# Order of side steps and evictions, gate softplus, compressed attention and the 2o3 turnover in a two-block kernel

## The reference, cut to what matters

```python
p_cmp = jax.nn.softmax(jnp.where(cmp_mask, s_cmp, NEG_INF), axis=-1) * cmp_mask
o_cmp = jnp.einsum('bhgsi,bihd->bshgd', p_cmp.astype(v_cmp.dtype), v_cmp)
o = g[..., 0, :] * o_cmp + g[..., 1, :] * o_sel + g[..., 2, :] * o_win
dt = jax.nn.softplus(dt_raw.astype(jnp.float32) + dt_bias.astype(jnp.float32))
h = h + mixed @ w_out[l]
h = h + (jax.nn.silu(v @ w_gate[l]) * (v @ w_up[l])) @ w_down[l]
```

```python
x = x + rms_norm(merged @ w_o[l], norm_mix_post[l])
h = rms_norm(x, norm_ffn_pre[l])
gate, up = jnp.split(h @ w_ffn_in[l], 2, axis=-1)
x = x + rms_norm((jax.nn.silu(gate) * up) @ w_ffn_down[l], norm_ffn_post[l])
```

## Time and profile before

| what | value |
|---|---|
| three runs, us | 2635.20, 2635.26, 2635.38; median 2635.26 |
| profiled execution, us | 2636.87, of which the profile's span is 2635.1 |
| TensorE (PE) | busy 2617.9 us, 99% of the span |
| VectorE (DVE) | busy 1483.2 us, 56% |
| ScalarE (ACT) | busy 1238.9 us, 47% |
| granted TensorE clock, mean | 0.999 |
| moved by DMA | 483.97 MB, 184 GB/s |

### The profile page before, as it was taken

One profiled execution on the slowest core, in us unless ns is written; L12 is line 12 of the kernel. 1 busy time (PEld: TensorE's weight loads), 2 busy tenths in 40 slices (PEclk: granted clock), 3 DMA queues, 4 the chain that ended last, 5 costly groups with the idle time before them and its releaser, 6 DMA issues.

```text
span 2635.1 us, 33219 instructions
## 1 busy us (share of the span) xinstructions
PE 2617.9 (99%) x13670; PEld 2238.4 (85%) x13670; DVE 1483.2 (56%) x1792; ACT 1238.9 (47%) x1577; POOL 0.2 (0%) x4
## 2 busy tenths in 40 slices
PE   9999999999999999999999999999999999999998
PEld 9989788888888888899899888888788888888887
DVE  6676765545454545566567644556655444555456
ACT  5565545443444444465454454444554444443443
POOL 0000000000000000000000000000000000000000
PEclk9999999999999999999999999999999999999999
DMA  8534445565555655556544435565565565565554
GB/s 306 164 122 144 151 148 199 189 191 193 191 188 191 193 193 187 191 182 211 185 157 154 151 130 190 185 234 187 167 211 186 192 194 189 191 191 192 190 193 144
DMA packets 132039, 483.97 MB, mean 184 GB/s; under 512 B 14704, under 2 KB 14960, under 8 KB 130832
## 3 DMA queue, kind: packets, MB, share of 16 engines
q1 hardware_dynamic: 131744, 481.70, 55.7%
q10 hardware_dynamic: 144, 0.15, 0.0%
HBM read 477.20 MB, written 4.19 MB: 183 GB/s over the span
## 4 chain that ended last, share of the span: by engine, by line
PE 98%; DVE 1%; ACT 1%; issue 0%; DVEq 0%
PE ps L415 96%; PE ps L419 2%; ACT W L989 0%; DVE W L1483 0%; DVE W L1886 0%; DVE scr L1483 0%; DVE wlo L1483 0%; DVE h L1486 0%; ACT whi L989 0%; ACT L989 0%; ACT xhi L989 0%; DVE xlo L1486 0%; ACT sm L989 0%; DVEq L2339 0%; DVE sm L1483 0%
## 5 line engine op out<-in xcount | busy, mean ns | idle before, releaser
L1483 DVE TENSOR_TENSOR wlo<-raw,whi 128x1024 fp32r<-128x1024 f32 x886 | 1082.1, 1223 | 1007.0 <-ACT whi L989 1002.9
L989 ACT ACTIVATE whi<-raw 128x1024 fp32r<-128x1024 f32 x886 | 935.7, 1058 | 1140.8 <-PE ps L415 1129.2
L415 PE MATMUL ps<-whi,xlo 128*128 128x512 f32 x2080 | 816.7, 393 | 0.0
L415 PE MATMUL ps<-wlo,xhi 128*128 128x512 f32 x2080 | 810.4, 390 | 0.0
L415 PE MATMUL ps<-whi,xhi 128*128 128x512 f32 x2080 | 810.3, 390 | 0.0
L415 PEld LDWEIGHTS ps<-wlo,xhi 128*128 128x128 f32 x2080 | 390.8, 188 | 82.0
L415 PEld LDWEIGHTS ps<-whi,xlo 128*128 128x128 f32 x2080 | 391.0, 188 | 79.8 <-issue 0.5
L415 PEld LDWEIGHTS ps<-whi,xhi 128*128 128x128 f32 x2080 | 391.0, 188 | 79.6 <-issue 0.5
L415 PE MATMUL ps<-whi,hlo 128*128 128x512 f32 x944 | 370.5, 392 | 0.0
L415 PE MATMUL ps<-wlo,hhi 128*128 128x512 f32 x944 | 367.5, 389 | 0.0
L415 PE MATMUL ps<-whi,hhi 128*128 128x512 f32 x944 | 367.3, 389 | 0.0
(11 more groups left out here) (130 smaller groups left out, 1013.2 us busy)
## 6 DMA issues: line engine op xcount, KB each, us to landing
raw<-in_gu SPq DMA_DIRECT2D x352, 512.0 KB, 3.8
raw<-in_w_in SPq DMA_DIRECT2D x256, 512.0 KB, 3.6
raw<-in_dn SPq DMA_DIRECT2D x176, 512.0 KB, 3.8
raw<-in_w_out SPq DMA_DIRECT2D x32, 512.0 KB, 3.6
raw<-in_w_up SPq DMA_DIRECT2D x32, 512.0 KB, 3.5
raw<-in_w_o SPq DMA_DIRECT2D x32, 512.0 KB, 3.9
raw<-in_cmp SPq DMA_DIRECT2D x8, 512.0 KB, 3.5
W<-in_wb SPq DMA_DIRECT2D x3, 1024.0 KB, 6.1
```

Of the source, the lines that this page charges most:

```text
L415: return e.matmul(o, l, r, start=start, stop=stop, skip_group_check=skip)
L989: return e.activation(o, i, f, **kw)
L1483: return e.tensor_tensor(o, a, b, op)
```

## The change

1. `walk()` on ScalarE and VectorE: the side step comes ahead of `after()` and `tick()`, no longer behind them. TensorE's `walk` keeps its order. Fox starts one step later on all three (`+ 6`).
2. `attention_T()` begins with an empty step on all three engines, and its transposes wait for `s_crd` 4 where it was 5; all that follows in the chain (`ssd`) is a step later.
3. `gates()`: 24 ticks pass between dt and softplus.
4. `compressed()`: the probabilities are multiplied with `t` in steps 5 and 6 (one more operation of 128x240), and in steps 9 and 10 the values in PSUM are added to `att_o` in one operation where there were two.
5. The turnover: `post(2, 0)` and `post(2, 1)` are issued in `turnover()` at tb 1, ahead of `quads_lo`; `posts()` keeps column block 3. The transposes of column blocks 2 and 3 move from behind units 0 and 2 of tb 1 to behind units 1 and 3.
6. The eviction of an `1x` item waits for `s_taps` as well.

```diff
@@ tensor, between_2fg0
-                elif (tb, u) in ((1, 0), (1, 2)):
+                elif (tb, u) in ((1, 1), (1, 3)):
                     c = 2 + u // 2
@@ tensor, attention_T (scalar and vector: the same yield)
             def attention_T():
+                yield
                 for k in range(0, 8, 2):
-                    tiles_T("h", HF["mix"] + k, 1024 + k * 128, scr, (s_crd, 4 + 1))
+                    tiles_T("h", HF["mix"] + k, 1024 + k * 128, scr, (s_crd, 4))
@@ tensor, scalar, vector: fox
-                while done[0] < end["2bf"] + 5:
+                while done[0] < end["2bf"] + 6:
@@ scalar and vector, walk
                         split_to(ahead(it["first"] + u))
                         done[0] += 1
+                        if side is not None:
+                            next(side, None)
                         if u == it["n"] - 1:
                             after(nm, it, pair_of(i))
                         tick()
-                        if side is not None:
-                            next(side, None)
@@ scalar, gates (vector: the same line ahead of its softplus)
                 m.then_inc(s_gs, 1)
+                yield from later(24)
                 yield from softplus(1, 32, 1)
@@ vector, after
                     on.wait_ge(s_tap0, 4 * n)
+                    on.wait_ge(s_taps, n)
                     mine()
@@ vector, turnover
                     if tb:
                         m.then_inc(ev["2o3"][0], 1)
+                        post(2, 0)
+                        post(2, 1)
@@ vector, compressed
-                        tt(ex, ex, bc(C("cmul")[:, tb * 15:tb * 15 + 15], 1, [P, 16, 15]), MUL).then_inc(s_cp, 1)
+                        own.up(tt(ex, ex, bc(C("cmul")[:, tb * 15:tb * 15 + 15], 1, [P, 16, 15]), MUL))
+                        mine()
+                        tt(ex, ex, bc(t, 2, [P, 16, 15]), MUL).then_inc(s_cp, 1)
...
-                            tt(rt, B("co", tb, gp).rearrange("p (h d) -> p h d", h=8), bc(t16c[tb][:, 8 * gp:8 * gp + 8], 2, [P, 8, 64]), MUL).then_inc(s_crd, 1)
-                            on.wait_ge(s_crd, 2 * tb + gp + 1)
-                            m = tt(att_o(tb, gp), att_o(tb, gp), rt, ADD)
-                            if (tb, gp) == (1, 1):
-                                m.then_inc(s_crd, 1)
-                            else:
-                                own.up(m)
+                            tt(att_o(tb, gp), att_o(tb, gp), B("co", tb, gp).rearrange("p (h d) -> p h d", h=8), ADD).then_inc(s_crd, 1)
@@ vector, posts
-                for c in (2, 3):
-                    post(c, 0)
-                    post(c, 1)
+                post(3, 0)
+                post(3, 1)
                 yield
```

More of the change, by code:

```diff
@@ L1925, in compressed @@
             def compressed():
-                rt = RT.rearrange("p (h d) -> p h d", h=8)
                 for i in range(11):
```

## The result

The changed kernel takes 2626.2 us (median of six runs, 2626.08 to 2626.36); the kernel before, run beside it, 2635.33 (six runs, 2635.20 to 2636.86). The ratio is 0.9962, 95% interval 0.9952 to 0.9973. The profiled executions took 2626.27 and 2636.87, with spans of 2624.5 and 2635.1.

A forecast was written before the change was run, and what follows sets the result against it. TensorE was taken to bound the kernel; 4.1 + 1.34 + 1.51 + 2.0 + 1.32 - 0.1 = 10.2 us off gave 2626.7 from the profiled 2636.87 and 2625.1 from the median 2635.26, range 2623.9 to 2629.2.

The forecast's parts named there:

- PE bounds, 8.0 us can go: Whole kernel: TensorE is busy 2617.9 of 2635.1 us; only 8.00 us of waits in five windows can go.
- The turnover, 4.1: Window 1888 to 1910: early posts remove PE's wait for h, 2.22 + 0.13, and 1.76 of slow clock.
- From the profiled execution to the median: Same sum of 10.2 us taken from profiled 2636.87 (2626.7) and from median 2635.26, lower with no profiler on (2625.1).
- Gates, 1.34: Units 36 and 37: moving softplus's two table loads saves 1.34 us, bounds 1.0 and 1.34; cost 0 in units 59 to 61.
- Side ahead of eviction, 1.51: First block, PE's wait at 139.75: the side step no longer stands behind the eviction, saving 1.38 + 0.13 us.
- Short units, 2.0 of 2.8: Window 177 to 205: 2.0 us of 2.78 saved, bounds 1.0 and 2.8; a wait of 0.5 to 0.7 stays.
- Compressed branch, 1.32: PE's wait at 272.70 goes, saving 1.19 + 0.13 us; the added multiplication costs 0, at worst 0.3.
- Forget, -0.1: ScalarE enters forget a unit earlier, in unit 397; wlo of unit 406 is tight: loss 0.1 us, bounds 0 and 1.0.
- The clock rival: Turnover: the clock stays low although the wait goes, 2625.1 + 1.8 = 2626.9 us; chance 0.12.
- The order was not the cause: At 139.75 and 177 to 205 banks decide, not the eviction, so edit 1 does nothing: 2628.6 us; chance 0.05.
- the two rules weighed: Skill pages: a drain of about 1.38 us on top of each table load; a clock monitor that runs on its own.

The follow-up runs named there:

- the order alone: Kernel before with the side step ahead of eviction and tick, fox a step later and edit 6's wait: 2629.0 us, ratio 0.9973.
- the order undone: Changed kernel with the side step of ScalarE and VectorE behind eviction and tick again, all other edits kept: 2630.79 us, ratio 0.9979.
- the better version: Changed kernel with the sum onto the output in attention's fin put off to the next step: 2625.85 us; with edit 3 also taken back, 2625.8.
- a third kernel: Changed kernel with softplus 15 ticks later instead of 24, so that it falls in the short units: 2631.09 us, ratio 0.9980.
- turnover alone: Kernel before with edit 5 alone (early posts, later transposes): 2632.83 us, eleven runs on one level, ratio 0.9987.

## Why the prediction was right or wrong

- *PE bounds, 8.0 us can go.* Right. 7.7 of the 8.00 went, nothing new came, and the hgrn, fox and feed-forward stretches gave and cost nothing (0.00 between units 80 and 626, and nothing behind unit 630).
- *The turnover, 4.1.* In the two profiled executions 4.03. The mechanism was right: the early posts took idle time of VectorE and cost nothing. But 1.6 of it is the slow clock, which by the levels comes in 35 of 59 runs. Of the edit's halves, the early posts alone give the whole gain; the late transposes alone leave 1.1 us of it.
- *From the profiled execution to the median.* This is the step that failed. I read the 1.6 us between 2636.87 and 2635.26 as the profiler's, and took off a sum with the slow clock's 1.76 in it from a median of runs that had none. From the lower level the sum is 2.4 + the rest, 9.0 us, and the lower levels of the two kernels are 9.1 apart. The forecast of 2625.1 came out only 1.1 too low because the other terms were 0.6 too small together (8.4 where 9.0 was measured); the two errors partly cancel, which is luck.
- *Gates, 1.34.* The size was right (1.33) and its cause was half: the table loads made the wait, but the order alone removes it, and with the order edit 3 is worth 0. I had given each wait to one edit and never asked whether another edit took the same one. The sum did not suffer from it, as all edits were made together; for the kernel with the order alone it was a microsecond off. That the pair costs nothing at its new place was right, as was that it needs cover: in the short units it costs 3.8.
- *Side ahead of eviction, 1.51.* 1.58, and the order undone gives it back. Right.
- *Short units, 2.0 of 2.8.* 2.33. The residue that I followed, 0.5 to 0.7 from `fin`, was there but smaller: 0.32 of idle time at 195.37, ahead of unit 56, and 0.36 when it was taken away. Going on from it gave the better version. The rest of those waits went entirely; ScalarE at 95% caused none.
- *Compressed branch, 1.32.* 1.38, by the order alone as much as by edits 2 and 4. The cost of the added multiplication is 0 with the new order, as said, and 0.23 with the old one. Not foreseen: with the new order the empty step is needed, or 0.27 is lost at unit 99; the kernel before does without it at no loss, and the order undone, which has it, loses 0.3 at unit 102.
- *Forget, -0.1.* 0.00. `wlo` of unit 406 ended at 1212.20, PE read it from about 1212.5: the margin is 0.3, not 0.
- *The rivals.* The clock rival was near the truth in its reason (the slow stretch does not follow the wait every time) and wrong in its direction: it is in the kernel before that it comes and goes, and in the changed kernel it came in none of six runs. *The order was not the cause* is answered by the order undone: 4.6 us came back.

Of the two rules weighed: the pair of table loads in units 60 and 61 cost nothing, as the rows had it, and not what the drain of the Trainium skill (ScalarE: Activation LUTs, What ACT_TABLE_LOAD costs) would have made of it; in every row here a load holds ScalarE 1.28 us. The two levels agree with a monitor that runs on its own, as the Trainium skill (TensorE: Matmul & The Clock Gate, Part 1) has it; no run shows more than this.

## What to carry to other kernels

When one engine is busy 99%, list its waits one by one, and for each ask which of the edits would remove it without the others: two sufficient edits are worth one, and undoing either of them alone shows nothing. Before a sum from a profiled execution is taken off a median, look at the single runs for levels, and put the profiled execution on one of them. A matmul's start may be late by 0.16 us without any idle time in the profile; the starts of matmuls and the waits of the weight loads show it. On an engine that issues in order, an eviction that waits for the end of a unit goes behind whatever can already run, if its own reader is far away.

## What the runs showed of the hardware

The same wait of 2.22 us was followed by 3.4 us at 1.2 GHz in one trace and by none in two others; the levels of the runs say that both happen with one and the same kernel, though no kernel has a trace of each. The low clock set in 1.2 us after the end of that wait, and 1.6 us after the end of one of 2.39 in a third kernel. Waits of 0.8 to 1.4 us were never followed by it in a trace. What decides from one execution to the next is open. Taking the wait away also took the spread from the runs: from 2.0 us between the lowest and highest of 59 to 0.4 of eleven (turnover alone) and 0.3 of six (changed kernel).
